# A hybrid attention and state-space layer: the attention output stored and split one step earlier, the branch product and the merge gates reordered

## The reference

```python
h = rms_norm(x, norm_gain)
q, k, v, z_a, z_s, xbc, dt_raw, gate_pre = split(h @ w_in)
o_a = window_attention(q, k, v, ...)              # 16 heads, window of 128
branch_a = (o_a * silu(z_a)) @ w_attn_proj
y_s = ssd_mixer(xbc, dt_raw, ...)                 # chunked scan, width 2048
y_s = rms_norm(y_s * silu(z_s), ssd_norm_gain)
branch_b = y_s @ w_ssd_proj
g_a, g_b = split(sigmoid(gate_pre + b_gate))
x = x + (g_a * branch_a + g_b * branch_b) @ w_out
```

## Time and profile before

| | |
|---|---|
| median of 3 runs | 1396.08 us (1394.50 to 1396.41) |
| the profiled execution, its own time | 1399.94 us |
| its span, first to last instruction | 1398.1 us |
| PE busy | 1353.0 us, 97% |
| DVE, ACT, POOL busy | 58%, 44%, 42% |
| mean granted clock of PE | 0.991 of full speed |

### The profile page before, as it was taken

One profiled execution on the slowest core, in us unless ns is written; L12 is line 12 of the kernel. 1 busy time (PEld: TensorE's weight loads), 2 busy tenths in 40 slices (PEclk: granted clock), 3 DMA queues, 4 the chain that ended last, 5 costly groups with the idle time before them and its releaser, 6 DMA issues.

```text
span 1398.1 us, 20354 instructions
## 1 busy us (share of the span) xinstructions
PE 1353.0 (97%) x7096; PEld 1082.6 (77%) x7096; DVE 810.9 (58%) x947; ACT 613.4 (44%) x1148; POOL 582.4 (42%) x338
## 2 busy tenths in 40 slices
PE   5899999999999999999999999999989999999899
PEld 5877777888888777778787787778867888788787
DVE  5876777766776375646455664756456454466311
ACT  5654435544545362525254544444357633333110
POOL 3634555544554343233323333332237665543321
PEclk9999999999999999999999999999989999999999
DMA  7333453433222576667868575858486365434331
GB/s 222 143 98 106 149 167 106 167 118 120 90 105 105 168 146 207 148 203 158 200 157 204 157 221 135 235 141 214 130 301 231 115 210 184 177 128 177 132 105 60
DMA packets 173673, 221.66 MB, mean 159 GB/s; under 512 B 7760, under 2 KB 136016, under 8 KB 173376
## 3 DMA queue, kind: packets, MB, share of 16 engines
q1 hardware_dynamic: 137808, 172.64, 43.3%
q10 hardware_dynamic: 35728, 48.37, 9.5%
q0 software_dynamic: 96, 0.13, 0.0%
HBM read 152.57 MB, written 63.31 MB: 154 GB/s over the span
## 4 chain that ended last, share of the span: by engine, by line
PE 76%; DMA 9%; issue 6%; DVE 4%; POOL 3%; ACT 2%; SPq 0%; ACTq 0%; POOLq 0%; DVEq 0%
PE F L186 32%; PE F L963 27%; DMA sb_early<-x_d 7%; PE F L1858 3%; PE M L1858 3%; PE M L1159 2%; POOL sb_res L1687 1%; PE M L1203 1%; PE F L1197 1%; PE F L1190 1%; PE F L1173 1%; PE M L1197 1%; PE M L1190 1%; POOL sb_whl L198 1%; DMA sb_early<-x 1%
## 5 line engine op out<-in xcount | busy, mean ns | idle before, releaser
L186 PE MATMUL F<-sb_xb,sb_whl 128*128 128x512 f32 x1536 | 376.1, 402 | 2.5 <-POOL sb_whl L198 2.5
L186 PEld LDWEIGHTS F<-sb_xb,sb_whl 128*128 128x128 f32 x1536 | 286.6, 188 | 77.0 <-issue 10.4
L198 POOL TENSOR_TENSOR sb_whl<-sb_wst,sb_whl 128x1024 fp32r<-128x1024 f32 x64 | 161.8, 2530 | 383.5 <-ACT sb_whl L195 383.0
L186 PE MATMUL F<-sb_X,sb_whl 128*128 128x512 f32 x1104 | 259.8, 397 | 1.1 <-POOL sb_whl L198 1.1
L186 PEld LDWEIGHTS F<-sb_X,sb_whl 128*128 128x128 f32 x1104 | 207.8, 188 | 52.8 <-issue 1.7
L963 PE MATMUL F<-sb_tv,sb_whl 128*128 128x512 f32 x1008 | 243.5, 397 | 2.3 <-DVE sb_acc L764 2.3
L963 PEld LDWEIGHTS F<-sb_tv,sb_whl 128*128 128x128 f32 x1008 | 190.0, 189 | 49.4 <-issue 2.7
L418 POOL TENSOR_TENSOR sb_whl<-sb_acc,sb_whl 128x512 fp32r<-128x512 f32 x103 | 145.9, 1424 | 137.4 <-ACT sb_whl L475 137.4
L963 PE MATMUL F<-sb_xb,sb_whl 128*128 128x512 f32 x756 | 186.4, 399 | 1.8 <-DVE sb_part L754 1.8
L963 PEld LDWEIGHTS F<-sb_xb,sb_whl 128*128 128x128 f32 x756 | 142.3, 189 | 40.3 <-issue 5.0
L195 ACT ACTIVATE sb_whl<-sb_wst 128x1024 fp32r<-128x1024 f32 x64 | 67.4, 1055 | 185.7 <-DMA sb_wst<-w_units 80.0
(11 more groups left out here) (223 smaller groups left out, 1759.2 us busy)
## 6 DMA issues: line engine op xcount, KB each, us to landing
sb_wst<-w_units SPq DMA_DIRECT2D x64, 512.0 KB, 6.1
sb_acc<-cs_d SPq DMA_DIRECT2D x8, 2048.0 KB, 22.5
sb_wst<-w_units SPq DMA_DIRECT2D x12, 1024.0 KB, 5.1
x_d<-sb_res ACTq DMA_DIRECT2D x24, 512.0 KB, 2.6
sb_acc<-w_units SPq DMA_DIRECT2D x10, 1024.0 KB, 5.1
sb_early<-x_d SPq DMA_DIRECT2D x8, 1024.0 KB, 9.0
sb_acc<-ecs_d SPq DMA_DIRECT2D x16, 512.0 KB, 24.6
z_d<-sb_res ACTq DMA_DIRECT2D x16, 512.0 KB, 12.0
```

Source lines behind the costliest of these rows:

```text
L186: last = nc.tensor.matmul(bank, weight(slot, wp, k), act(ap, k, half), start=(k == 0 and wp == 0 and ap == 0), stop=(k == NK - 1 and wp == 1))
L198: return nc.gpsimd.tensor_tensor(weights(slot, 1), raw_unit(slot), weights(slot, 0).bitcast(f32), ALU.subtract)
```

## The change

Four edits, all between the last tile of block 2 and the end of the third pass:

1. ACT stores `zo` in `o_d` ahead of `unit_out(1)` in the last tile; SP's last tile is written out behind its loop and loads slices 4, 5, 6, 0, 1, 2, 3 between the weights of two units.
2. The slices go in the order 4, 5, 6, 0, 1, 2, 3, 7 everywhere. POOL makes the low parts of 4 and 5; DVE makes that of 6 inside the tile, ahead of `y_take(3)`, and the others behind it. ACT makes the high parts of 4, 5, 6 ahead of `take_half(6)`.
3. In the first pass the branch product goes ahead of the low part of y.
4. In the third pass gate B is made a turn ahead: ACT's sigmoid for the next turn stands between `merged_high` (half 0) and `high`, POOL's scaling for the next turn ahead of `low`.

```diff
+        O_ORDER = (4, 5, 6, 0, 1, 2, 3, 7)
+        O_POOL = (4, 5)
...
-                for n in range(3, 6):
+                for n in range(3, 5):
                     load_w(sp, B2 + n, 4, j)
+                if last_tile:
+                    sp.wait_ge(o_stored, 16 * (NT + 1))
+                    sp.wait_ge(xd_ready, 4 * NT + 1)
+                    for k in O_ORDER[:NK - 1]:
+                        sp.dma_start(X1[:, 1, k, :].bitcast(f32), o_d[k]).then_inc(o_in[k], 16)
+                load_w(sp, B2 + 5, 4, j)
...
+        def o_low(k):
+
+            nc.vector.wait_ge(o_hi, O_ORDER.index(k) + 1)
+            nc.vector.tensor_tensor(X1[:, 1, k, :], X1[:, 1, k, :].bitcast(f32), X1[:, 0, k, :].bitcast(f32),
+                                    ALU.subtract).then_inc(act_lo, 1)
...
                 y_out(1)
                 y_out(0)
+                if last_tile:
+                    o_low(O_ORDER[2])
...
                 take_half(3)
+                if last_tile:
+                    act.wait_ge(oT_ready, 2 * NT + 2)
+                    act.dma_start(o_d[:, :, ds(j * P, P)].rearrange("n p t -> p n t"), zo[:]).then_inc(o_stored, 16)
                 unit_out(1)
...
                 if last_tile:
-                    act.wait_ge(yg_done, 4 * NT + 1)
-                    for k in range(NK):
+                    for k in O_ORDER:
+                        if k == O_ORDER[2]:
+                            act.wait_ge(wT_ready, 4 * NT)
+                        if k == O_ORDER[3]:
+                            take_half(6)
+                            act.wait_ge(yd_done, 2 * NT)
+                        if k == O_ORDER[7]:
+                            act.wait_ge(yg_done, 4 * NT + 1)
                         act.wait_ge(o_in[k], 16)
...
-            sp.wait_ge(o_stored, 16 * (NT + 1))
-            sp.wait_ge(xd_ready, 4 * NT + 1)
-            for k in range(NK - 1):
-                sp.dma_start(X1[:, 1, k, :].bitcast(f32), o_d[k]).then_inc(o_in[k], 16)
...
-            with nc.gpsimd.Fori(0, 4) as i:
-                for s in range(2):
-                    pool.wait_ge(gateB_ready, i * 2 + (s + 1))
-                    nc.gpsimd.tensor_tensor(gate[:, s, :], gate[:, s, :], ms, ALU.mult).then_inc(gr_ready, 1)
-                    low(pool, B3 + 18 + s, 2, i)
+            scaled_gate(0, 0)
+            with nc.gpsimd.Fori(0, 3) as i:
+                scaled_gate(i, 1)
+                low(pool, B3 + 18, 2, i)
+                scaled_gate(i + 1, 0)
+                low(pool, B3 + 19, 2, i)
...
+            def merge_turn(i, s, following):
+                merged_high(i, s, 0)
+                if following:
+                    merge_gate(*following)
+                high(act, B3 + 18 + s, 2, i)
+                merged_high(i, s, 1)
...
                 for s in range(2):
-                    gate_and_low(X0, 0, i, s)
+                    gated_y(X0, 0, i, s)
                     dve.wait_ge(gateA_ready, i * 2 + (s + 1))
                     dve.wait_ge(unit_done, i * 4 + 2 * (B3 + s + 1))
                     nc.vector.tensor_tensor(acc_tile(i, s), acc_tile(i, s), pair3(s), ALU.mult).then_inc(pair3_free[s], 2)
+                    y_low(X0, 0, i, s)
...
+            pe.wait_ge(y_taken, 4 * NT + 1)
             unit3(0, X1, 0, free=False, tiles=0)
```

More of the change, by code:

```diff
@@ L1095, in load_bc, with tile_loads @@
                 sp.dma_start(bc[:], x_d[16:24, :, ds(at_j, P)].rearrange("n p t -> p n t")).then_inc(bc_in, 16)
-            def tile_loads(j, at_j, first):
+            def tile_loads(j, at_j, first, last_tile=False):
                 sp.wait_ge(sc_done, j * 4 + 1)
@@ L1480, in _ @@
                 else:
+                    act.wait_ge(oT_ready, at(2, 4))
+                    act.dma_start(o_d[:, :, ds(j * P, P)].rearrange("n p t -> p n t"), zo[:]).then_inc(o_stored, 16)
+                    take_half(6)
                     take_half(7)
@@ L1722, in merged_high, with merge_gate @@
                 nc.scalar.activation(split_tile(X0, 0, i, s)[:, to], acc_tile(i, s)[:, to], ACT.Copy).then_inc(m_hi, 1)
-            with nc.scalar.Fori(0, 4) as i:
-                for s in range(2):
-                    act.wait_ge(merge_in[s], i * 32 + 32)
-                    nc.scalar.activation(gate[:, s, :], gate[:, s, :], ACT.Sigmoid,
-                                         bias=C("b_gate", 8, 16)[:, ds(i * 2 + s, 1)]).then_inc(gateB_ready, 1)
-                    merged_high(i, s, 0)
-                    high(act, B3 + 18 + s, 2, i)
-                    merged_high(i, s, 1)
+            def merge_gate(i, s):
+                act.wait_ge(merge_in[s], i * 32 + 32)
+                nc.scalar.activation(gate[:, s, :], gate[:, s, :], ACT.Sigmoid,
+                                     bias=C("b_gate", 8, 16)[:, ds(i * 2 + s, 1)]).then_inc(gateB_ready, 1)
+            def merge_turn(i, s, following):
[4 more added lines that the diff above has]
+                merged_high(i, s, 1)
+            merge_gate(0, 0)
+            with nc.scalar.Fori(0, 3) as i:
+                merge_turn(i, 0, (i, 1))
+                merge_turn(i, 1, (i + 1, 0))
+            merge_turn(3, 0, (3, 1))
+            merge_turn(3, 1, None)
             with nc.scalar.Fori(0, 3) as i:
@@ L1744, in gate_and_low, with y_low @@
                 nc.vector.tensor_tensor(y, y, tile(X, 0, i, s), ALU.mult).then_inc(gated, 1)
+            def y_low(X, q0, i, s):
+                y, n = tile(X, 1, i, s), q0 + s + 1
                 dve.wait_ge(act_hi, i * 2 + n)
@@ L1748, in gate_and_low @@
                                                tile(X, 0, i, s), ALU.mult, ALU.subtract).then_inc(act_lo, 1)
-            for k in range(NK):
-                if k not in O_POOL:
-                    dve.wait_ge(o_hi, k + 1)
-                    nc.vector.tensor_tensor(X1[:, 1, k, :], X1[:, 1, k, :].bitcast(f32), X1[:, 0, k, :].bitcast(f32),
-                                            ALU.subtract).then_inc(act_lo, 1)
+            for k in O_ORDER[3:]:
+                o_low(k)
             with nc.vector.Fori(0, 4) as i:
                 for s in range(2):
-                    gate_and_low(X0, 0, i, s)
+                    gated_y(X0, 0, i, s)
                     dve.wait_ge(gateA_ready, i * 2 + (s + 1))
```

34 lines of the change are left out of this document (20 added, 14 removed).

## The result

| | before | changed |
|---|---|---|
| median of 6 runs each | 1396.24 us (1392.90 to 1397.21) | 1388.17 us (1385.87 to 1390.49) |
| the profiled execution, its own time | 1399.94 us | 1389.83 us |
| its span | 1398.1 us | 1388.0 us |
| mean granted clock of PE | 0.991 | 0.994 |

The ratio of the times is 0.9948 with a 95% interval from 0.9932 to 0.9964.

The account below looks back on a forecast made before the run. PE was taken as the bound, busy 97% of the span. 1.0 - 0.2 + 2.2 = 3.0 us won: 1399.94 to 1396.9 for the profiled execution, 1393.1 for the median, which lay 3.9 lower; range 1389.5 to 1397.5.

Parts of the forecast that it names:

- Place A: Start of block 3, up to its third unit: chain of waits 3.5 us shorter, less 2.5 for the clock, 1.0 won.
- DVE's low part of slice 6: Ahead of `y_take(3)` in the last tile: it would lengthen the chain to the third unit by 0.8 us (0 to 3).
- the rival in which the early store holds up the weights: Last scan products wait for weights delayed by the `o_d` store: -3 us on Place A, 1396.5 to 1399; chance 0.08.
- The price of 7.68 for slice 7: Load of slice 7 ahead of the third unit: 3.7 us (3.5 to 7.7) instead of 7.68, winning 4.0.
- The clock behind the pause: After one 6.8 us wait ahead of the third unit, PE at the lower clock for 4 to 7 us: 2.5 lost.
- the clock holds: Rival: behind the pause the clock holds or returns at once; sum 5.5 us won, 1390.6; chance 0.16.
- The first pass: Branch product ahead of the low part of y: 0.2 us lost (0 to 1), at slice 7 of the second pass.
- Place B: Between the first output product's halves: the 3.51 us wait goes, less a new 1.3 us: 2.2 won (0 to 3.8).
- The new wait: Ahead of the fourth merge unit, ended by POOL's `low`: PE waits 1.3 us, once.
- The slower rival: Merge hangs on its loads, from 6.8 us a load; at 8 some 5 us slower, 1400.5; chance 0.10.

Follow-up runs that it names:

- e12: The changed kernel with only the store of the attention output (`o_d`) put back behind `unit_out(2)`; one run, 1394.32 us.
- e2: The kernel before with only the early store and loads of the attention output and the new slice order; 1392.64 us, ratio 1.0005.
- e6: The changed kernel with the next turn's gate in the merge behind `high` on ACT and behind `low` on POOL; one run, 1387.30 us.
- e11: The changed kernel, unedited, profiled and timed again; 1386.30 us, ratio 0.9948 to the kernel before.
- e5: The changed kernel with 24 more matmuls, into a bank nobody reads, behind the second unit; one run, 1383.92 us.
- e10: The changed kernel with the edits of e5 and e6 together; 1383.99 us, ratio 0.9930 to the kernel before.
- e3: The kernel before with only the first pass's branch product put ahead of the low part of y; 1393.41 us, ratio 1.0006.
- e1: The kernel before, unedited, profiled and timed again; 1392.64 us, ratio 0.9998.
- e4: The kernel before with only gate B of the third pass made a turn ahead; 1387.56 us, ratio 0.9969.
- e9: The changed kernel with e6's order, the last `y_d` store before slice 7's high part, and one weight unit before early gate and `z_d` loads; 1383.74 us, ratio 0.9923.
- e7: The changed kernel with the first turn's gate and `z_d` loads, then the next weights, not waiting for the last stores; one run, 1388.61 us.
- e8: e7 with the order of e6; 1389.33 us, ratio 0.9974 to the kernel before.

## Why the prediction missed

**Place A, the chain: right, on the one profile.** It said 3.5 us shorter and the third unit at 1049.2, which is 35.05 us behind the last half unit; it came 34.23 behind. Slice 7's load took 3.50 where 3.7 was said. Two terms inside were off and nearly cancel: the gate store gave back nothing (4.97 against 4.90, said to be 0.3 less) and `z_d` 1.40 us, of which 1.25 went to the slower issue of the `y_d` load. What is left of the difference, 0.8, is the next point.

**DVE's low part of slice 6: 0, not 0.8.** Counted from the last half unit's start, which came 4.57 us earlier than in the profile of before, the store was issued when it was said to be (989.65, there 994.2), but the seven loads left at 995.69, there 1000.3 and not 1003: the store did not have to stand behind the weights. ACT's high parts were earlier by as much, and the low part of slice 6 was done before PE's last scan product. DVE's rows of the changed kernel:

```profile
1004.79 3.05 DVE L1280 TENSOR_TENSOR sb_X<-sb_X 128x1024 fp32r<-128x1024 f32 x1 [3.16 <-ACT sb_X L1501]
1009.86 0.69 DVE L1346 TENSOR_TENSOR sb_acc<-sb_acc,M 128x512 f32<-128x512 f32 x1 [2.02 <-PE M L1205]
```

It was held up (3.05 us, with POOL's work beside it) and there were still 2.02 us to spare. That also settles the rival in which the early store holds up the weights: ACT's wait for them was 9.10 us and ended 16.6 us ahead of the last half unit, where it was 12.72 and ended 13.1 ahead. e12 shows what lies at the far end: with late loads A is 7 us longer, more than the 3 of the prediction's bound. The prediction's 2.37 us for a held-up subtraction came from a row of L1775, a multiplication of half the size; the 3.05 stands against 1.23 for the same subtraction undisturbed.

**The price of 7.68 for slice 7 is one execution's.** The four kernels with the old handoff show 7.68, 6.99, 5.43 and 5.29 us, so A gains 2.7 us on average and not 4.3. The prediction had bounds for the new load (3.5 to 7.7), and none for the old one, whose spread it couldn't see in one profile.

**The clock behind the pause: right in kind, somewhat over in size.** One pause of 5.98 us (6.8 said), a clock of 0.50 behind it, 1.6 us lost in the profile; over e2, e6, e11 and the changed kernel 1.5 to 2.6 against 2.5 said. e5 shows that the idle time causes it, and e10 shows it again. Net, place A gives 0.9 us by the average traces (2.7 less 1.8) and 1.0 was said. That this agrees is luck: the chain was put 0.8 too high and the clock's price 0.7 too high. The rival "the clock holds" is out.

**The first pass: right.** 0.2 said; e3 0.08, e5 0.09.

**Place B: the step that failed.** It said 3.5 less 1.3, so 2.2 us with bounds 0 and 3.8, "The 3.51 us at B left it at 1.00". The new wait was well worked out. In the changed profile it is 1.15 us ahead of the fourth unit (0.64 to 1.2 in other kernels), and the steps to it stand as said: ACT's sigmoid, held for the load, POOL's scaling, then `low`:

```profile
1232.46 1.15 ACT L1755 ACTIVATE sb_res<-sb_res,sb_cst 128x1024 f32<-128x1024 f32 x1 [2.57 <-DMA sb_part<-a_d]
```
```profile
1233.69 2.41 POOL L1707 TENSOR_TENSOR sb_res<-sb_res,sb_ssd_sb 128x1024 f32<-128x1024 f32 x1 [8.98 <-ACT sb_res L1755]
1236.06 2.83 POOL L198 TENSOR_TENSOR sb_whl<-sb_wst,sb_whl 128x1024 fp32r<-128x1024 f32 x1
```

What was mis-sized is what the removed gaps cost. From start to start of the matmuls, the gaps of 0.30 and 3.51 us cost 4.3 us (a merge of 90.46 against 90.00 with no gap, an output product of 93.22 against 89.37), and 1.4 to 1.5 us more were lost at the lower clock in three profiles of four, 1.1 on average. The new wait takes 1.1 on average of three. B gives 4.2 us, more than its upper bound, since the bound took the clock at 1.00 from the single execution that had it so; on that execution alone B would have given 2.9.

That DVE waits "3.54 or so in a turn" for the scaling was also only half right. The waits are of two lengths, 2.1 and 3.5 us, and the long ones fall in the turns in which ACT's sigmoid has a table load of 1.28 us ahead of it. The merge of the kernel before has four of these loads (ACT_TABLE_LOAD at L1727), that of the changed kernel one. The prediction doesn't mention them.

**The sum.** By places it is 2.7 less 1.8, plus 4.2, so 5.1 us; taken directly, the whole stretch has 380.6 us in before and e1 and 375.3 in the changed kernel and e11, 5.3 less. The forecast had 3.0. Timed, the gain was 7.3 us, the same ratio twice, with intervals that begin at 5.0. So of the 4.3 us that the forecast lacks 2.0 belong to B, and some 2 are in no place. With B right the forecast would have been 1391.1, within the range; the other 2 us took the time out of it. (By the prediction's own terms the range should have begun at 1389.0: 3.5 less 0.2, plus 3.8. That would not have held the result either.)

These 2 us stay open, but the traces narrow them down. From the start of the last tile's 64x64 matmuls on PE (959.32 in before, 954.86 in the changed kernel) to the last half unit it is 54.7 or 54.8 us in thirteen traces and 55.2 in e4, so edits 1 and 2 change nothing there; from the last matmul to the end it is 3.6 us in before, e1, the changed kernel and e11 alike. What is left lies ahead of the last tile, whose instructions the change leaves as they were. There PE waits for loads of `x_d` in some executions and not in others (5.8 us in before, 0.6 in e1, 3.3 in the changed kernel, 0.7 in e11), and the last half unit begins between 1006.1 and 1014.2 us in the four kernels with the old handoff and between 1005.0 and 1009.6 in the others. Chance fits that; the ratio that came twice speaks against it, and no run decides. SP's last tile, written out behind its loop, is an unlikely cause: e2 has it and timed at 1.0005.

That the profile stood 3.9 above the median, with a load wait and a clock loss near 573 us that e1 lacks, was taken into account by taking the 3.9 off.

**What the merge didn't do.** The slower rival wanted loads of 6.8 us or more. In the changed profile ACT's waits for `a_d` were six, of 9.7 us in all, and none reached PE after the fourth unit:

```profile
ACT sb_res L1755 <- DMA sb_part<-a_d: 9.7, 6, 2.6
```

## What to carry to other kernels

Before a gap of a few microseconds in front of PE is priced by one profile, look at it in a second execution: its length repeated within 0.1 us here, but what the clock did behind it did not, and that was worth 40% of the gap. When a chain of transfers ends such a pause, ask which store on it the loads ahead would slow before moving loads up; issuing the store first won at A (2.5 us, e9) what the early loads lost (2.1 and 2.6, e7 and e8). If a pause can't be removed, matmuls into an unused bank can buy its clock loss back, so long as they end before the wait does: here 24 of them, 5.6 us in a pause of 6, won 1.6 us of the passes in e5 and e10 alike. Fewer were not tried.

## What the runs showed of the hardware

- A gap of 3.45 to 3.51 us at the same place left the granted clock at 1.00 in one profile; in e1 it was at 0.50 for 3.3 us behind it, and e2 and e3 lost the same 1.4 to 1.5 us. A pause of 3.37 us in e9 cost 2.6 us in the passes, as much as 6.39 us in e11 (2.6) and more than 5.98 us in the changed kernel (1.7). Over all eight profiles with an unfilled pause, from 3.37 to 8.62 us long, the price was 1.5 to 1.7 us in five and 2.6 to 2.7 in three (e8, e9, e11), and didn't follow the length.
- The store of `y_d` took 5.1 us in before, the changed kernel and e11, 8.24 us when issued early, right behind the load of slice 7 (e9), and 13.10 to 13.54 us with four loads issued within 1.8 us ahead of it and a unit of weights right behind it (e7, e8).
- With POOL's operations back to back, DVE operations of two on-chip operands were held up one after the other: 2.47 us (L1817) and then 2.78 us (L1819) where 0.69 is usual.
